# Rotation in twenty quarter blocks with two buffers, and the gate blocks' Silu behind the third snapshot

## The reference, cut to what matters

```python
proj = x @ w_in[l]
aq, ak, av, dqkv, dbeta, da, dz, gates = jnp.split(proj, SPLIT_POINTS, axis=-1)
aq = apply_rope(aq.reshape(B, S, N_Q_HEADS, HEAD_DIM), cos, sin)
ak = apply_rope(ak.reshape(B, S, N_KV_HEADS, HEAD_DIM), cos, sin)
y_attn = banded_sink_attention(aq, ak, av, attn_sink[l])
dqkv = jax.nn.silu(causal_depthwise_conv(dqkv, conv_w[l]))
o_dn = gated_delta_rule(dq, dk, dv, beta, g)                # scan over 16 chunks of 64
o_dn = o_dn * jax.nn.silu(dz...)                            # dz: the four "gate blocks" of the change
merged = gate_a * (y_attn @ w_branch_attn[l]) + gate_b * (y_dn @ w_branch_dn[l])
x = layer_norm(DEEPNORM_ALPHA * x + merged @ w_out[l], ...)
h = jnp.square(jax.nn.relu(x @ w_up[l]))
x = layer_norm(DEEPNORM_ALPHA * x + h @ w_down[l], ...)
```

## Time and profile before

| | us |
|---|---|
| three runs, median (lowest, highest) | 1401.55 (1396.18, 1402.2) |
| the profiled execution | 1397.5 |
| its span | 1395.7 |
| TensorE busy | 1373.6 (98%) |
| VectorE, ScalarE, GpSimd busy | 1025.1, 607.8, 177.7 |

### The profile page before, as it was taken

The page is one execution under the profiler, slowest core; times in us unless marked ns, Lnnn a source line. Parts: engine busy times, 40 slices in busy tenths (PEclk is TensorE's granted clock), DMA queues, the critical chain, the costliest instruction groups (busy, mean ns, idle before and its releaser), DMA issues.

```text
span 1395.7 us, 21990 instructions
## 1 busy us (share of the span) xinstructions
PE 1373.6 (98%) x8400; PEld 1140.1 (82%) x8400; DVE 1025.1 (73%) x1890; ACT 607.8 (44%) x1306; POOL 177.7 (13%) x163
## 2 busy tenths in 40 slices
PE   9999998999999999999999999999999999999997
PEld 8788887787888888788888888888888888888885
DVE  7999885855888888655358796766665777777778
ACT  4655534432344444532113455455554544444540
POOL 4322322230000000235800000000000000000002
PEclk9999999999999999999999999999999999999999
DMA  6232344675443542244612153444335875555422
GB/s 215 91 121 106 121 162 157 223 230 172 120 108 99 133 111 56 80 151 153 231 81 110 52 190 121 166 166 166 151 126 220 302 240 176 161 165 180 128 69 120
DMA packets 123497, 206.83 MB, mean 148 GB/s; under 512 B 40865, under 2 KB 61569, under 8 KB 121089
## 3 DMA queue, kind: packets, MB, share of 16 engines
q1 hardware_dynamic: 113312, 183.93, 40.1%
q10 hardware_dynamic: 10080, 21.50, 4.1%
HBM read 142.92 MB, written 62.47 MB: 147 GB/s over the span
## 4 chain that ended last, share of the span: by engine, by line
PE 87%; DVE 6%; DMA 4%; SPq 2%; issue 1%; ACT 0%; ACTq 0%; POOL 0%; DVEq 0%; POOLq 0%
PE ps L2590 6%; PE ps L2588 6%; PE ps L2589 6%; PE ps L2209 6%; PE ps L2571 6%; PE ps L2572 6%; PE ps L2573 6%; PE ps L2157 5%; PE ps L2158 5%; PE ps L2159 5%; PE ps L2275 4%; PE ps L2096 4%; PE ps L2097 4%; PE ps L2095 4%; PE ps L2465 2%; PE ps L2469 2%
## 5 line engine op out<-in xcount | busy, mean ns | idle before, releaser
L2588 PE MATMUL ps<-thi,shi 128*128 128x512 f32 x416 | 161.8, 389 | 0.0
L2589 PE MATMUL ps<-tlow,shi 128*128 128x512 f32 x416 | 161.8, 389 | 0.0
L2590 PE MATMUL ps<-thi,slow 128*128 128x512 f32 x416 | 161.8, 389 | 0.0
L943 ACT ACTIVATE thi<-b 128x512 fp32r<-128x512 f32 x104 | 65.5, 630 | 108.0 <-PE ps L2590 108.0
L1979 DVE TENSOR_TENSOR tlow<-b,thi 128x512 fp32r<-128x512 f32 x104 | 71.8, 690 | 52.7 <-ACT thi L943 52.6
L2589 PEld LDWEIGHTS ps<-tlow,shi 128*128 128x128 f32 x416 | 78.1, 188 | 16.3
L933 POOL TENSOR_TENSOR zt<-zt,ln2gb 128x256 f32<-128x256 f32 x4 | 3.4, 852 | 690.7 <-ACT zt L1394 690.7
L2590 PEld LDWEIGHTS ps<-thi,slow 128*128 128x128 f32 x416 | 78.1, 188 | 16.2
L2588 PEld LDWEIGHTS ps<-thi,shi 128*128 128x128 f32 x416 | 78.1, 188 | 16.0
L1972 DVE TENSOR_TENSOR slow<-sraw,shi 128x512 fp32r<-128x512 f32 x104 | 71.3, 686 | 21.7 <-ACT shi L943 20.6
L943 ACT ACTIVATE shi<-sraw 128x512 fp32r<-128x512 f32 x104 | 65.1, 626 | 31.6 <-DMA zt<-xpark 16.4
(11 more groups left out here) (445 smaller groups left out, 3827.5 us busy)
## 6 DMA issues: line engine op xcount, KB each, us to landing
raw<-in_wblk SPq DMA_DIRECT2D x55, 512.0 KB, 4.5
sraw<-hpark SPq DMA_DIRECT2D x104, 256.0 KB, 2.8
hpark<-hq SPq DMA_DIRECT2D x16, 1024.0 KB, 4.9
b<-in_wblk SPq DMA_DIRECT2D x64, 256.0 KB, 3.5
wraw<-in_wblk SPq DMA_DIRECT2D x30, 512.0 KB, 4.0
hpark<-hq SPq DMA_DIRECT2D x16, 768.0 KB, 4.9
park<-cb ACTq DMA_DIRECT2D x34, 256.0 KB, 3.9
park<-cacc ACTq DMA_DIRECT2D x12, 512.0 KB, 3.2
```

The costliest lines, as they stand in the source:

```text
L943: cp = lambda o_, i_: act.activation(o_, i_, ACT.Copy)
L2588: mm(outp, shi[s][:, ts], thi[m][:, :], start=first, stop=False, skip_group_check=True)
L2589: mm(outp, shi[s][:, ts], tlow[m][:, :], start=False, stop=False, skip_group_check=True)
L2590: return mm(outp, slow[s][:, ts], thi[m][:, :], start=False, stop=final, skip_group_check=True)
```

## The change

1. The rotation runs in twenty units of a quarter block (128x256), in two buffers of `rraw` and `rswp`, with a semaphore for each. The units go quarter by quarter over the five blocks. The table is loaded per quarter, in two buffers too.
2. `ROPE_AT` gives each turn of VectorE three units (turn 7 one, turn 13 four). The first stands behind the A12 low part, the second ahead of `combine_in(n, 1)`, the third at the end of the turn. In turn 13 the last one stands behind the last `combine_in`.
3. SyncE loads units 0 and 1 in its turn 8. After that each unit has in the queue its store and, directly behind, the load of the unit two further on, which waits for that store to have landed. All units of VectorE's turn n-1 are served in SyncE's turn n.
4. For n = 9 and 10 `store_pair(n-1)` with its Silu stands behind the third snapshot instead of the second.
5. One semaphore less (`g_dif` becomes a second count of `g_exp`).

```diff
-        rtab = at("rtab", 96, [P, 2, HALF], extra=16512)
-        rraw = at("rraw", 96, [P, HALF], extra=16512 + 4096)
-        rswp = at("rswp", 96, [P, HALF], extra=16512 + 6144)
+        rtab = [at(f"rtab{e}", 96, [P, 2, S // 4], extra=16512 + 2048 * e) for e in range(2)]
+        rraw = [at(f"rraw{e}", 96, [P, S // 4], extra=16512 + 4096 + 1024 * e) for e in range(2)]
+        rswp = [at(f"rswp{e}", 96, [P, S // 4], extra=16512 + 6144 + 1024 * e) for e in range(2)]
...
-        ROPE_AT = {7: (None, 0), 8: (1, 2), 9: (3, 4), 10: (5, 6), 11: (7, None), 12: (8, None), 13: (9, None)}
+        ROPE_AT = {7: (None, None, 0), 8: (1, 2, 3), 9: (4, 5, 6), 10: (7, 8, 9), 11: (10, 11, 12), 12: (13, 14, 15), 13: (16, 17, 18, 19)}
...
             def rope_load(u):
-                if u:
-                    sp.wait_ge(rope_out, 16 * u)
+                if u >= len(ROPE):
+                    return
+                if u >= 2:
+                    sp.wait_ge(rope_out, 16 * (u - 1))
...
-                before, (first, second) = ROPE_AT.get(n - 2, (None, None))[1], ROPE_AT.get(n - 1, (None, None))
-                if before is not None:
-                    rope_store(before)
-                if first is not None:
-                    rope_load(first)
-                if n > DEC0 + 1:
-                    dec_load(2 * (n - DEC0) - 1)
-                if first is not None:
-                    rope_store(first)
+                if n == ROPE0:
+                    rope_load(0)
+                    rope_load(1)
+                for k, u in enumerate(ROPE_AT.get(n - 1, ())):
+                    if u is not None:
+                        rope_store(u)
+                        rope_load(u + 2)
+                    if k == 0 and n > DEC0 + 1:
+                        dec_load(2 * (n - DEC0) - 1)
                 if n > DEC0:
                     dec_load(2 * (n - DEC0))
-                if second is not None:
-                    rope_load(second)
...
                 in_snap(n, 1)
-                if n > N_DN // 2:
+                if n > N_DN // 2 and not B_DZ < 2 * n < B_GATE + 1:
                     store_pair(n - 1)
...
                 in_snap(n, 2)
+                if n > N_DN // 2 and B_DZ < 2 * n < B_GATE + 1:
+                    store_pair(n - 1)
...
                 in_lo(n + 1, "A11", "A22", "A12")
+                rope(n, 0)
                 combine_in(n, 0)
...
-                if ROPE_AT.get(n, (None,))[0] is not None:
-                    rope(ROPE_AT[n][0])
+                rope(n, 1)
                 combine_in(n, 1)
...
                 in_lo(n + 1, "S3")
-                if ROPE_AT.get(n, (None, None))[1] is not None:
-                    rope(ROPE_AT[n][1])
+                rope(n, 2)
```

More of the change, by code:

```diff
@@ L388, in hybrid_block @@
         g_eg = sem("g_eg")
-        g_dif = sem("g_dif")
         g_all = sem("g_all")
@@ L403, in hybrid_block @@
         dec_in = sem("dec_in")
-        rope_in = sem("rope_in")
+        rope_in = [sem(f"rope_in{e}") for e in range(2)]
         rope_out = sem("rope_out")
@@ L499, in hybrid_block @@
         waited = sem("waited")
-        ROPE = [(0, 0), (1, 0), (2, 0), (3, 0), (4, 0), (0, 1), (1, 1), (2, 1), (3, 1), (4, 1)]
-        ROPE_AT = {7: (None, 0), 8: (1, 2), 9: (3, 4), 10: (5, 6), 11: (7, None), 12: (8, None), 13: (9, None)}
-        ROPE_TAB = [n for n, (_, h) in enumerate(ROPE) if n == 0 or ROPE[n - 1][1] != h]
+        ROPE = [(i, q) for q in range(4) for i in range(5)]
+        ROPE_AT = {7: (None, None, 0), 8: (1, 2, 3), 9: (4, 5, 6), 10: (7, 8, 9), 11: (10, 11, 12), 12: (13, 14, 15), 13: (16, 17, 18, 19)}
         ROPE0, DEC0 = 8, 10
-        ROPE_IN = [16 * (5 * (n + 1) + sum(m <= n for m in ROPE_TAB)) for n in range(len(ROPE))]
+        RQ = S // 4
+        ROPE_IN = [16 * sum(5 + (m % 5 == 0) for m in range(n % 2, n + 1, 2)) for n in range(len(ROPE))]
         def rope_cols(n):
-            i, h = ROPE[n]
-            return B_Q + i, slice(PAD + h * HALF, PAD + (h + 1) * HALF)
+            i, q = ROPE[n]
+            return B_Q + i, slice(PAD + q * RQ, PAD + (q + 1) * RQ)
         T_ADDS = ("T1", "T2", "T3", "T4")
@@ L619, in rope_load @@
             def rope_load(u):
-                if u:
-                    sp.wait_ge(rope_out, 16 * u)
[L623 to L630, removed]
+                if u >= len(ROPE):
+                    return
+                if u >= 2:
+                    sp.wait_ge(rope_out, 16 * (u - 1))
+                e, (b, sl) = u % 2, rope_cols(u)
+                i, q = ROPE[u]
+                sp.wait_ge(ub_out[q // 2], (16, 48, 48, 80, 80)[i])
+                if i == 0:
+                    sp.dma_start(rtab[q % 2][:, :, :], A["rope"][:, :, sl]).then_inc(rope_in[e], 16)
+                sp.dma_start(rraw[e][:, :], park[b, :, sl]).then_inc(rope_in[e], 16)
+                for g in range(4):
+                    r = g ^ 1
+                    sp.dma_start(rswp[e][32 * g:32 * g + 32, :], park[b, 32 * r:32 * r + 32, sl]).then_inc(rope_in[e], 16)
             def rope_store(u):
@@ L1550, in dec_args, with rope @@
                 tt(d[:, 0, :, :], d[:, 0, :, :], bh(msk(M_ML)), ALU.add).then_inc(dec_arg, 1)
-            def rope(u):
-                dve.wait_ge(rope_in, ROPE_IN[u])
-                tt(rraw[:, :], rraw[:, :], rtab[:, 0, :], ALU.mult)
-                chain(tt(rswp[:, :], rswp[:, :], rtab[:, 1, :], ALU.mult))
-                tt(rraw[:, :], rraw[:, :], rswp[:, :], ALU.add).then_inc(rope_ok, 1)
+            def rope(n, k):
+                u = ROPE_AT.get(n, (None, None, None))[k]
+                if u is None:
+                    return
+                e, tab = u % 2, rtab[ROPE[u][1] % 2]
+                dve.wait_ge(rope_in[e], ROPE_IN[u])
+                tt(rraw[e][:, :], rraw[e][:, :], tab[:, 0, :], ALU.mult)
+                chain(tt(rswp[e][:, :], rswp[e][:, :], tab[:, 1, :], ALU.mult))
+                tt(rraw[e][:, :], rraw[e][:, :], rswp[e][:, :], ALU.add).then_inc(rope_ok, 1)
             for n in range(N_IP - 1):
```

11 lines of the change are left out of this document (7 added, 4 removed).

## The result

| | before | changed |
|---|---|---|
| median (lowest, highest), us | 1401.03 (1396.18, 1402.2) | 1441.89 (1439.47, 1442.67) |
| profiled execution, its span | 1397.5, 1395.7 | 1442.4, 1440.4 |
| mean granted clock | 0.997 | 0.983 |

The ratio is 1.0305, with a 95% interval of 1.0286 to 1.0324: 40 to 45 us slower. (The median before is of four runs; the table ahead of the prediction had three of them.) The prediction was 1433, range 1415 to 1450.

What follows compares the result with a forecast made beforehand. TensorE was the bound, its waits due to ScalarE's and SyncE's queue order; afterwards a SyncE ring of 23.0 us a turn would put the first dqs transpose at 352.5, 35.2 us later. Added to 1397.5: 1433, range 1415 to 1450.

Steps and rivals of the forecast that it cites:

- Silu behind the third snapshot: ScalarE's Silu work in pair 9 moves behind the snapshot; TensorE's wait at 224.19 goes, 2.05 us, at no cost.
- the ring: SyncE's weights, VectorE's first unit, x, third unit, x, next weights: 23.0 us a turn against 19.04 on TensorE.
- x = 4.5: In SyncE's queue, a unit's store, its landing and the load behind it take 4.5 us; bounds 3.6 and 5.0.
- Third unit ahead of the weights, L9 = 197.3: In SyncE's queue pair 9's weights wait behind turn 7's unit and are issued at 197.3, ten microseconds later than before.
- The step from the weights to the first unit: From weights' issue, 8.3 us to the end of VectorE's A12 split, then 1.2 us to rotate the first unit.
- The dec term: VectorE's third unit waits for decp and decay work in two turns: 8.4 us instead of 4.5 each.
- Behind L14, 27.2: From SyncE's last weights issue (L14, 325.3) through the last units and dqs load to TensorE's first dqs transpose, 352.5.
- The clock costs nothing in the ring: TensorE restarts cold after each new hole, but its slower products only fill the next hole: no added time.
- Behind the first transpose: From the first dqs transpose to L2268 the distance stays as before, 11.7 us, and nothing is given back later.
- Rival 1: SyncE reaches the weights in time, the 7.2 us of waits go, transposes 3.6 us late: 1394; chance 6%.
- Rival 4: TensorE's clock losses at five holes and the stand before the transposes are not hidden: 11 us more, 1444; chance 5%.
- Rivals 2 and 3: Rival 2, quick ring: x 3.9, two long turns 24.3, 1417, 16%. Rival 3, congested ring: x about 6, 1452, 13%.

Runs made afterwards that it cites:

- silu_only: The kernel before with only store_pair of pairs 8 and 9 (Silu and stores) moved behind the third snapshot: 1395.38 us, ratio 0.9983.
- third_late: The changed kernel, with SyncE serving the third unit of each VectorE turn behind the next pair's weights: 1414.97 us, ratio 1.0122.
- after_dec_ahead: The changed kernel with decp's loads moved ahead of the first and third units' stores in SyncE's turns 11 to 13: 1434.02 us, ratio 1.0256.
- pool_fill: The changed kernel with GpSimd filling buffers with zeros instead of computing the sums from pair 9 on: 1431.05 us, ratio 1.0234.
- third_late_hoist: third_late with the scan's first loads (dqk, dqs, dv) issued ahead of the stores of units 18 and 19: 1414.53 us, ratio 1.0119.

## Why the prediction was right, and where it was short

The time fell in the range, 9 us above the number. Step by step:

- **What bounds the kernel**: right. The loss lay in SyncE's queue, with TensorE idle in front of S4 and dqs. (It stood another 2.4 us before the fillers, at 342.59, which the wait for dqs covers.)
- **Silu behind the third snapshot**: the number was right, the way to it only in part. Predicted 2.05 us and no cost; silu_only measured 2.4. The hole went as said, but another grew by 1.8 us, and the 1.9 us of clock that came back in its place were not in the prediction: the agreement is in part luck. In the ring it should be worth nothing, since the time there is not TensorE's; no run took the step out of the changed kernel.
- **x = 4.5**: right. Between two stores in the queue lay 3.9 to 5.9 us, and in the turn shown 4.39, 4.42 and 5.12. The store alone lands in 1.7 us. Issued directly behind a unit's loads it took up to 3.6 (the range of landings of these stores is 1.7 to 3.6, median 1.8).
- **Third unit ahead of the weights, L9 = 197.3**: right within 1.1 us, and third_late shows that this place is the largest single cause, 27 of 43 us.
- **The step from the weights to the first unit, 8.3 + 1.2 = 9.5**: this is the term that was mis-sized. It measured 11.0, 10.7, 11.1, 11.2 and 11.0, together 7.5 us more in five turns, of the 9.7 by which these ran over. The 1.2 for the unit was 2.25 each time, since its first pass took 1.50 us. The 8.3 came out at 8.4 to 8.9 by two errors: VectorE's A22 split began 5.5 to 6.0 us behind the issue in place of 7.0 (209.13 to 216.13 in the trace of before), and the two stretched splits, 2.9 us in place of 1.3, took that back and more. The 8.3 was read from a turn in which GpSimd's first sum began only at 217.04, released by TensorE, so the splits had VectorE to themselves nearly to their end. In the changed kernel the weights are what both engines wait for, so they start together in every turn. The trace of before had the sign, and I took the short row for the rule:

```profile
201.02 1.82 DVE L1478 TENSOR_TENSOR ipS1l<-ipS1r,ipS1h 128x512 fp32r<-128x512 f32 x1 [4.37 <-POOL ipS2r L881]
...
201.00 1.30 POOL L885 TENSOR_TENSOR s4raw<-raw,ipS2r 128x512 f32<-128x512 f32 x1
...
217.04 1.54 POOL L875 TENSOR_TENSOR ipS1r<-raw 128x512 f32<-128x512 f32 x1 [9.68 <-PE ps L2159]
```

- **The dec term, +3.9 in two turns**: right; after_dec_ahead gained 8 (3.9 and 3.3 in the two turns).
- **Weights to S4, 7.93**: 6.6 to 7.1 in the changed kernel. It places the holes, but has no part in the sum of 35.2, so nothing came of it.
- **Behind L14, 27.2**: 27.3. It came out by luck, through two errors that cancel. Unit 16 was rotated 7.2 us behind L14 in place of 5.3: decp took 4.5 us to land in place of 3.5, and the passes beside GpSimd's splits for the next stage took 0.81 to 1.14 us in place of 0.42 (338.5 to 343.9). And unit 19, the last, was rotated 2.9 us behind its load's last issue (350.9 to 353.8) in place of 4.5.
- **The clock costs nothing in the ring**: the forecast holds, though no run isolates it. After the hole at 254.01 the granted clock was 0.50 for two microseconds, the 1.2 GHz level, and likewise behind the other four. By the prediction each new hole would start at this level: four of the five did, and behind the one of 3.64 us the clock fell a microsecond later. The product took longer, and since SyncE's queue sets the turns, the next hole should be shorter by it. The windows of the changed kernel (us; busy times; granted clock third from the end):

```profile
254.00:256.00 2.00, 1.99 (x5) 1.61 (x6) 2.00 (x3) 2.00 (x4) 1.92 (x2) 0.50 0.00 0
256.00:258.00 2.00, 2.00 (x8) 1.60 (x7) 1.97 (x4) 0.77 (x1) 0.99 (x1) 0.75 0.19 70
258.00:261.00 3.00, 3.00 (x15) 2.48 (x14) 2.96 (x8) 2.01 (x3) 0.00 (x0) 1.00 0.93 347
```

- **Behind the first transpose, "what it was"**: short by the 0.8 us shown with the result. The granted clock was 0.50 there from 361 to 365, behind the stand of 10.39 us, and 1.00 in the same place before (317 to 320). That the clock is the cause is not tested.

Rival 1 (the change does what it says) is out by every row. Rival 4 asked for 11 us of clock losses that count: at most the 0.8 behind the last stand was found. Rivals 2 and 3 differed from the forecast in x, which sat at the middle, and rival 2 also in the long turns, which came (29.8 and 30.0 us).

## What to carry to other kernels

A second buffer hides no landing when each load stands in the queue directly behind the store that it waits for (no run here tried the quarters with one buffer): count how often a queue waits per turn, add the issues, and compare with the turn of the bound engine. When a change makes two engines wait for the same transfer, price their first passes as if they ran side by side, not by the row in which each ran alone. And count a wait together with the clock that it may cost: the Silu step paid in clock what it didn't pay in waits. Before a load is moved out of a full queue, look what else stands in it; weights, decp and dqs took turns as the next late thing here.

## What the runs showed of the hardware

- **VectorE and GpSimd take turns.** A VectorE pass over two operands in the on-chip buffer ends only behind the sum that GpSimd was at: 1.25 to 1.77 us in place of 0.69. GpSimd pays too, 1.61 us for a sum in place of 1.27. Beside a fill of GpSimd, which reads nothing, the same passes took 0.69 and 0.42. The Trainium skill says this (SBUF — State Buffer, section "SBUF: two separate sides"): the two engines share a pair of ports under an exclusive lock that is held for a whole instruction, and a VectorE operation with two operands there is hit only by a GpSimd operation that reads there. This trace and pool_fill agree in both halves. With three sums in the way of three passes (+0.56, +1.08 and +1.08 us, the durations measured here less the plain ones) the plain steps of pool_fill, 8.0 to 8.8 us, become 10.7 to 11.5; the changed kernel measured 10.7 to 11.2. Added to the 9.5 of the prediction they would have given 12.2, since the 9.5 held about a microsecond too much elsewhere.
- **Where the clock falls after a hole.** It was at 0.50 from the restart behind the holes of 3.49, 4.17, 6.40 and 8.83 us. Behind others it was high at the restart and 0.50 a microsecond or so later: behind 2.07 us (third_late, 240.23: 1.00 until 241, then 0.59), 1.91 in the kernel before (0.99 until 243, then 0.50), and also behind 3.64 (0.85 from 229 to 230, then 0.50) and 3.74 (third_late_hoist, 262.80: 1.00 until 263, then 0.83, then 0.50). Behind 1.62 (pool_fill, 227.12), 1.89 (the kernel before, 224.19), 1.99 and 2.18 us (silu_only, 262.85 and 50.98) it stayed at 1.00. So the length of the hole alone doesn't settle it. The first matmul's duration shows the restart, 0.77 or 0.47 us, but not what comes next.
- **The landing of a small store varies.** From the issue of a 128 KB store to the next step it took 1.7 us after a pause of the queue, 1.8 to 3.6 directly behind the five loads of a unit (3.6 at 211.50, next step at 215.14; 2.2 at 237.42), and 4.7 to 6.7 directly behind two weight loads (third_late, 234.13 and 303.22). What decides within these ranges no run shows.
